# A two-layer encoder trunk on one core: the close of the last tile but one laid over its whole phase, the first norm's parameters expanded two pairs sooner, and the opening norm fed by a broadcast behind x

## The reference, cut to what matters

```
h = layer_norm(x, ln_in_g, ln_in_b)                       # x: 256 tokens x 1024
for i in range(2):
    mix = token_mixers(h, w_in[i], w_out[i], ...)         # differential attention + indexed sparse attention
    h = layer_norm(ALPHA * h + mix, ln1_g[i], ln1_b[i])
    r = ALPHA * h + peer_ffn(h, ...)                      # per token: 8 heads x top 16 of 16384 experts
    gate = sigmoid(r @ ple_wg[i] + ple_bg[i])
    r = r + gate * (p[i] @ ple_wp[i])
    h = layer_norm(r, ln2_g[i], ln2_b[i])
# peer_ffn, per token: act = gelu(u_tab[eidx] . x);  out = sum_k g_k * act_k * v_tab[eidx_k]
```

## Time and profile before

| | |
|---|---|
| median of 3 runs | 1705.87 us (1705.35 to 1707.51) |
| the profiled execution: time | 1710.65 us |
| the profiled execution: span of the core | 1708.8 us |
| PE busy | 1273.0 us (74%) |
| DVE busy | 1071.7 us (63%) |
| POOL busy | 578.6 us (34%) |
| ACT busy | 464.4 us (27%) |
| moved by DMA | 670.38 MB, of which the gathers 536.90 MB |
| mean granted clock of PE | 0.87 |

### The profile page before, as it was taken

How to read it: one execution, slowest core, us unless ns; L and a number is a source line. 1 busy time by engine, 2 the same in 40 slices (tenths; PEclk the granted TensorE clock), 3 DMA queues, 4 the chain that set the end, 5 groups by cost and what they waited for, 6 DMA issues and landing times.

```text
span 1708.8 us, 17975 instructions
## 1 busy us (share of the span) xinstructions
PE 1273.0 (74%) x6232; PEld 590.4 (35%) x6232; DVE 1071.7 (63%) x2754; ACT 464.4 (27%) x1270; POOL 578.6 (34%) x516
## 2 busy tenths in 40 slices
PE   8988767786878798685765979678785885555566
PEld 6655533231542274132531337232352221010112
DVE  1458669664768765555858785663676877555553
ACT  1323223352223323422222422242121342111112
POOL 0003233444322432443334332333333435444430
PEclk9999978988898899798998979968796998767879
DMA  7859999999999999999999999998999989999992
GB/s 254 293 211 407 418 416 402 415 421 418 419 417 419 418 415 417 418 417 419 411 417 421 402 410 415 418 394 341 421 418 418 421 328 420 422 421 421 422 421 116
DMA packets 110522, 670.38 MB, mean 392 GB/s; under 512 B 12240, under 2 KB 12880, under 8 KB 44640
## 3 DMA queue, kind: packets, MB, share of 16 engines
q0 software_dynamic: 73728, 536.90, 76.1%
q1 hardware_dynamic: 36528, 132.20, 19.9%
q10 hardware_dynamic: 176, 0.13, 0.0%
HBM read 668.14 MB, written 1.05 MB: 392 GB/s over the span
## 4 chain that ended last, share of the span: by engine, by line
DMA 40%; PE 32%; DVE 11%; issue 10%; POOL 4%; ACT 3%; POOLq 0%; ACTq 0%; DVEq 0%
DMA rows<-uv_dram,rows_of 34%; PE acc L1231 13%; PE bank L1020 7%; PE bank L1034 6%; DMA wring<-wmix_dram 6%; DVE rows L980 6%; POOL rows L472 4%; ACT dg L644 1%; PE bank L1139 1%; PE bank L1208 1%; PE bank L1131 1%; PE bank L1029 1%; ACT gel L640 1%; DVE i L711 0%; DVE i L702 0%
## 5 line engine op out<-in xcount | busy, mean ns | idle before, releaser
L472 POOL DMA_INDIRECT rows<-uv_dram,rows_of x512 | 578.4, 1130 | 1089.2 <-PE acc L1231 866.5
L980 DVE CUSTOM_DVE_ANT_0 rows<-rows,hx 128x1024 f32<-128x1024 f32 x512 | 621.4, 1224 | 484.3 <-DMA rows<-uv_dram,rows_of 474.0
L1231 PE MATMUL acc<-rows,dg 128*32 128x512 f32 x2048 | 611.2, 733 | 364.9 <-ACT dg L644 364.4
L1231 PEld LDWEIGHTS acc<-rows,dg 128*32 128x32 f32 x2048 | 115.0, 123 | 769.1 <-ACT dg L644 524.1
L640 ACT ACTIVATE gel<-dots 128x2 f32<-128x2 f32 x256 | 51.8, 202 | 817.0 <-DVE dots L980 807.1
L1034 PE MATMUL bank<-wring,xT 128*128 128x512 f32 x384 | 175.3, 601 | 14.4 <-DMA wring<-wmix_dram 13.0
L1020 PE MATMUL bank<-xT,wring 128*128 128x128 f32 x1216 | 148.6, 284 | 10.3 <-DMA wring<-wmix_dram 6.9
L1020 PEld LDWEIGHTS bank<-xT,wring 128*128 128x128 f32 x1216 | 143.6, 198 | 22.1 <-issue 8.1
L644 ACT ACTIVATE dg<-idg,gel 128x32 f32<-128x32 f32 x512 | 136.6, 314 | 24.6 <-ACT gel L640 1.1
L1020 PE MATMUL bank<-qT,wring 128*128 128x128 f32 x896 | 119.4, 295 | 17.8 <-DMA wring<-wmix_dram 17.1
L1020 PEld LDWEIGHTS bank<-qT,wring 128*128 128x128 f32 x896 | 113.0, 208 | 39.9 <-issue 20.4
(11 more groups left out here) (159 smaller groups left out, 932.5 us busy)
## 6 DMA issues: line engine op xcount, KB each, us to landing
wring<-wmix_dram SPq DMA_DIRECT2D x204, 512.0 KB
wring<-wclose_dram SPq DMA_DIRECT2D x30, 512.0 KB
rows<-uv_dram,rows_of POOLq DMA_INDIRECT x512
rows<-wmix_dram SPq DMA_DIRECT2D x8, 512.0 KB, 11.0
rows<-prm_dram SPq DMA_DIRECT2D x2, 1024.0 KB, 10.2
fixed<-fixed_dram SPq DMA_DIRECT2D x1, 576.0 KB, 7.9
res<-x_dram SPq DMA_DIRECT2D x1, 512.0 KB, 4.1
hx<-x_dram SPq DMA_DIRECT2D x1, 512.0 KB, 6.2
```

Source lines behind the costliest of these rows:

```text
L472: pool.indirect_dma_start(out=rows[:, slot, :], out_offset=None, in_=uv_d[phase // TILES], in_offset=bass.IndirectOffsetOnAxis(ap=rows_of[ ...
L980: V.tensor_tensor_reduce(out=rows[:, s, 0:D], in0=rows[:, s, 0:D], in1=hx[:, c, :], scale=1.0, scalar=0.0, op0=ALU.mult, op1=ALU.add, accu ...
L1231: ins = MM(acc[BT * c:BT * c + BT, 512 * i:512 * i + 512], dg[:, s, :], rows[:, s, D + 512 * i:D + 512 * i + 512], start=False, stop=False ...
```

## The change

It has three parts.

Opening. `lnin` (four matmuls, three selectors ahead of it) is gone. The broadcast of the opening norm's gain and shift into `rows[:, 0]`, 1 MB, which stood after `dv1`, is now the second DMA of SP, behind x and ahead of all weights; `embed0` reads it. ACT does the square root of `embed0` before the selectors (`rows`), which are now those of `par` and of the first norm. Two parts with no use of their result are new on PE: `wake`, eight 128x128 matmuls as soon as the identity is there, and `fill`, three 128x512 matmuls between `mix1b` and `h1T`.

First norm's parameters. `gb0` and `gb1` of a mixing run stand at pairs 28 and 29 instead of 30 and 31, and their copy goes to `sc` instead of `probsT`. `mix1a` stands one pair later, behind `mT1`.

Close of CLOSE[2]. In phase 4 each of its pair numbers is taken times three (`close_last`). Both closes of layer 1 now copy `ple` from PSUM into `val`; before, CLOSE[2]'s was read from PSUM. CLOSE[3]'s own `ple` stands at pair 4 instead of 1.

```
-    ("mT0", 30, 31, None), ("gb0", 30, 31, None), ("gb1", 31, 32, None), ("mix0a", 32, None, None), ("mix1a", 32, None, None),
-    ("mT1", 33, 34, None), ("mix0b", 34, None, None), ("mix1b", 35, None, None),
+    ("gb0", 28, 29, None), ("gb1", 29, 30, None), ("mT0", 30, 31, None), ("mix0a", 32, None, None),
+    ("mT1", 33, 34, None), ("mix1a", 33, None, None), ("mix0b", 34, None, None), ("mix1b", 35, None, None),
...
-LAST_EARLY = [("ple", 1, 2, None), ...
+LAST_EARLY = [("ple", 4, 5, None), ...
...
+def close_last(p):
+    return 3 * p
...
-            lay(k, CLOSE_PLAN, CLOSE[k - 2])
+            lay(k, CLOSE_PLAN, CLOSE[k - 2], close_last if k == RUNS else int)
...
             sp.dma_start(res[:], x_d[0]).then_inc(x0_landed, 16)
+            sp.dma_start(rows[:, 0, :], prm_d[P_IN:P_IN + 2, :].rearrange("a d -> (a d)")[None, :].broadcast_to([128, 2 * D])
+                         ).then_inc(lnin_landed, 16)
...
+            def gb_half(run, i):
+                return flat(sc, 512 * i, 512 * i + 512) if run.stage == "mix" else quarter(probsT, i)
...
-                    gain = P_LN1 + 2 * run.layer if n else P_IN
-                    chooser(S_G, gain)
-                    chooser(S_B, gain + 1)
-                    chooser(S_PAR, P_PAR + run.layer).then_inc(rows_ready, 1)
+                    chooser(S_PAR, P_PAR + run.layer)
+                    chooser(S_G, P_LN1 + 2 * run.layer)
+                    chooser(S_B, P_LN1 + 2 * run.layer + 1).then_inc(rows_ready, 1)
...
-                        take(run, name, quarter(probsT, int(name[2])))
+                        take(run, name, gb_half(run, int(name[2])))
...
-                if part == "ple" and run is CLOSE[3]:
+                if part == "ple" and run.layer:
                     for i in range(2):
-                        take(run, f"ple{i}", val[:, 0, 512 * i:512 * i + 512])
+                        take(run, f"ple{i}", val[:, run.tile, 512 * i:512 * i + 512])
...
-                    given = [bank_of(run, f"lnin{i}")[0][:] for i in range(4)]
-                    norm_a([half_of(res, 0), half_of(res, 1)], h, given[0:2], [full_at(run, f"lnin{i}") for i in range(2)])
...
+                    norm_a([half_of(res, 0), half_of(res, 1)], h, params(rows[:, 0, :], 0), [(lnin_landed, 16)])
+                    norm_b(h, params(rows[:, 0, :], D), h_ready)
...
+                if part == "wake":
+                    pe.wait_ge(ident_landed, 16)
+                    for i in range(8):
+                        MM(acc[:, 0:128], ident, ident, start=True, stop=True, skip_group_check=True)
+                if part == "fill":
+                    for i in range(3):
+                        MM(acc[:, 0:512], ident, fixed[:, 128:640], start=True, stop=True, skip_group_check=True)
```

More of the change, by code:

```diff
@@ L174 @@
 ]
-LAST_EARLY = [("ple", 1, 2, None), ("bias", 58, None, None), ("warm0", 60, None, None), ("warm1", 61, None, None),
+LAST_EARLY = [("ple", 4, 5, None), ("bias", 58, None, None), ("warm0", 60, None, None), ("warm1", 61, None, None),
               ("warm2", 62, None, None), ("warm3", 63, None, None)]
@@ L181 @@
 ]
-START_PE = ("lnin T par idx dq0 dq1 dk0 dk1 iw ds0 ix sq0 sq1 dv0 dv1 dpt sk0 dpv sk1 ss0 sv0 sv1 mT0 mix0a mix1a spt0 spt1 spv mT1 "
-            "mix0b mix1b h1T pq0a ps0 pq1a init hx0 ps1 hx1 perm0 pq2a hx2 hx3").split()
-START_ACT = ("rows embed0 T par idx dq1 dk1 iw ix exps0 exps1 sq1 dv1 dpt dpv sk1 rms sexp0 sexp1 sv1 mT0 spt0 spt1 mT1 embed1 n1a "
+START_PE = ("wake T par idx dq0 dq1 dk0 dk1 iw ds0 ix sq0 sq1 dv0 dv1 dpt sk0 dpv sk1 ss0 sv0 sv1 mT0 mix0a mix1a spt0 spt1 spv mT1 "
+            "mix0b mix1b fill h1T pq0a ps0 pq1a init hx0 ps1 hx1 perm0 pq2a hx2 hx3").split()
+START_ACT = ("embed0 rows T par idx dq1 dk1 iw ix exps0 exps1 sq1 dv1 dpt dpv sk1 rms sexp0 sexp1 sv1 mT0 spt0 spt1 mT1 embed1 n1a "
              "h1T pq0a ps0 C0a pq1a hx0 ps1 hx1 hx2 hx3").split()
@@ L859, in part_of @@
                 if part in ("n1a", "n1b"):
-                    buf = rows[:, 1, :] if n == 0 else gb
+                    buf = rows[:, 1, :] if n == 0 else flat(sc, 0, 2 * D)
                 if part == "n1a":
@@ L889, in part_of @@
                     bk, taken = bank_of(run, f"ple{i}")
-                    if run is CLOSE[3]:
+                    if run.layer:
                         dve.wait_ge(*taken_at(run, f"ple{i}"))
-                        V.tensor_tensor(half_of(mixed, i), half_of(mixed, i), half_of(val[:, 0, :], i), ALU.mult).then_inc(L.sem, L.one())
+                        V.tensor_tensor(half_of(mixed, i), half_of(mixed, i), half_of(val[:, run.tile, :], i), ALU.mult).then_inc(L.sem, L.one())
                         settle()
@@ L1047, in part_of @@
                     transposes(run, ["hT0", "hT1"], lambda c: src[:, T * c:T * c + T], [(ready, before + 1), (ready, before + 2)])
[L1048 to L1051, removed]
-                        bk, full = bank(run, name)
-                        MM(bk[:], selrow[:, S_G + i // 2, :], prm[:, 512 * (i % 2):512 * (i % 2) + 512], start=True, stop=True
-                           ).then_inc(full, 1)
+                if part == "wake":
[5 more added lines that the diff above has]
+                        MM(acc[:, 0:512], ident, fixed[:, 128:640], start=True, stop=True, skip_group_check=True)
                 if part == "par":
+                    if n == 0:
+                        pe.wait_ge(prm_landed, 16)
                     pe.wait_ge(rows_ready, n + 1 + max(0, n - 1))
```

2 lines of the change are left out of this document (removed), and 2 rows, old and new, of the table per.

## The result

The changed kernel takes 1692.16 us (median of 4 runs, 1690.59 to 1696.3) where the kernel before took 1705.61 (4 runs): ratio 0.992 (95% interval 0.99 to 0.994), 13.45 us less. The forecast was 1688.9, made of 17.0 us. The profiled execution of the changed kernel took 1696.3, the longest of its four; that of before (1710.65) lies above all four timed runs of before, which end at 1707.51.

What follows compares the result with a forecast made beforehand. DMA was taken as the bound, time being bytes over its rate plus its idle time. Savings of 7.5 + 6.5 + 3.0 = 17.0 us from the median of 1705.87 gave 1688.9, range 1677 to 1700.

Steps and rivals of the forecast that it cites:

- Opening, 7.5: Before the first gather: earlier broadcast, `fill` and `wake` together save 7.5 us.
- The broadcast, 4.5: Opening: broadcast behind x lands at about 7.4, transposes start at 9.7 instead of 14.23, 4.5 us earlier.
- `fill` 3.0: Before h1's transposes: matmuls in PE's idle time save 3.0 us on projection and transposes; bounds 0 and 3.0.
- `wake` 0: Start of PE: raising the clock could save up to 3.7 us; taken as 0, since PE idles again before the transposes.
- Parameters, 6.5: Phase 3: moving `gb0`, `gb1` earlier saves 6.5 of 10.9 us idle DMA; 4.9 at half clock, 10.9 at full.
- How it comes about: Phase 3: `spv` at clock 0.50 (7.09 us), then `gb0`, delay pair 30, and the DMA runs dry.
- Close, 3.0: Head of phase 4: spreading the close saves 3.0 of 9.6 us idle; two whole blocks leave 5.7 at full clock.
- a pair may come 2.5 us late: Price rule for POOL's gathers: a pair's delay up to 2.5 us costs nothing, each microsecond beyond costs one.
- more than that: Rival: `wake` raises the clock and `spv` runs at full clock, 27 us gained, 1679; chance 0.21.
- Only the opening pays: Rival: phase 3 falls back to 0.50 and phase 4's two whole blocks start cold, 1697; chance 0.16.
- the broadcast is late: Rival: broadcast lands at 11.4, the opening gives 3.5, sum 13, 1693; chance 0.07.
- Slower: Rival: all blocks of the spread close run at half clock, 25.6 us lost in phase 4, 1719; chance 0.04.

Runs made afterwards that it cites:

- open_only: The kernel before with only the opening's part of the change (broadcast behind x, `wake`, `fill`, ACT's order); 1697.26 us, ratio 0.9942.
- no_close: The changed kernel without the spread of the close in phase 4; 1697.16 us, ratio 0.9952.
- before_again: The kernel before, unchanged, profiled once more; 1704.05 us in one run.
- dose12: The changed kernel with 96 unused matmuls added to PE in the quiet part of phase 4, in 12 blocks of 8; 1690.02 us, ratio 0.9907.
- no_wake: The changed kernel without the `wake` matmuls ahead of the first transposes; 1692.09 us, ratio 0.9917.
- close_only: The kernel before with only the spread close of phase 4, the `ple` copy into `val` and CLOSE[3]'s `ple` at pair 4; 1699.48 us, ratio 0.9958.
- gb_late: The changed kernel with the first norm's parameters (`gb0`, `gb1`) back at pairs 30 and 31; 1692.41 us, ratio 0.9922.
- lean: split with the first norm's parameters back at pairs 30 and 31 and without `wake`; 1693.94 us, ratio 0.9931.
- split: The changed kernel with its close laid out so that no two blocks stand together, CLOSE[3]'s `ple` at pair 3; 1690.1 us, ratio 0.9908.
- no_fill: The changed kernel without the `fill` matmuls ahead of h1's transposes; 1693.89 us, ratio 0.9929.
- dose3: The changed kernel with the same 96 unused matmuls added to PE in phase 4, in 3 blocks of 32; 1748.33 us, ratio 1.0243.

## Why the prediction was right, and which terms were not

The medians of three kernels, each with one part more, split the gain: before 1705.61, open_only 1697.26, no_close 1697.16, changed kernel 1692.16. That is 8.35 for the opening, 0.1 for the parameters and 5.0 for the close, together 13.45; the prediction had 7.5, 6.5 and 3.0. (Against before of its own batch no_close gained 8.18, which would make the last two -0.2 and 5.3.) That the sum came so near is in part luck: one term was almost wholly wrong, and the two others made up for 2.9 of its 6.4 us.

**Opening, 7.5: right.** The broadcast, 4.5: measured 4.24 and, against before_again, 4.56 us (transposes at 9.99, 14.23 and 14.55); it landed at 7.77 where 7.4 was taken. `fill` 3.0, measured 2.7 by the first gather, 1.7 by the medians. `wake` 0: the medians agree, the mechanism only half. The transposes took 1.23 instead of 1.94 us in four of the eight profiles with `wake` and in none of the six without. Timeline of PE in dose12:

```profile
5.27 3.60 PE L1057 MATMUL acc<-fixed 128*128 128x128 f32 x16 [5.27 <-DMA fixed<-fixed_dram]
10.22 1.23 PE L1016 MATMUL bank<-fixed,h 128*128 128x128 f32 x8 [1.35 <-DVE h L700]
...
12.41 21.32 PE L1026 MATMUL bank<-xT,wring 128*128 128x128 f32 x176
```

By these durations the clock was up at the transposes (the granted clock tells nothing here: it reads 1.00 over the first 10 us in both kinds, even where the matmuls are slow), and the projections start 1.0 us earlier than at 13.44 and end 1.8 earlier. In the four such profiles they end at 33.6 to 33.7 us, in the six others with the early broadcast at 34.9 to 35.6. So in half of the profiles `wake` was worth 1.2 to 2 us of its upper bound of 3.7. That no_wake's median shows none of it stays unexplained. The Trainium skill ("TensorE: Matmul & The Clock Gate", Part 1) says that sustained activity releases the clock at a point that differs from run to run; these profiles agree with it. First gather, over the seven kernels with the whole opening: 115.33 to 120.45, mean 118.5; over the four without: 126.07 to 127.51, mean 126.7. That is 8.2 us, as the medians have it. The 5.6 between the two first profiles is low because the mixing block at 89 us took 8.83 us in one and 7.13 in the other; of the fourteen profiles only before, before_again and dose12 have 7.13.

**Parameters, 6.5: the failed term.** The step was "How it comes about: `spv` takes 7.09 us at clock 0.50": one execution was read as the kernel. With the parameters at pairs 30 and 31 `spv` took 7.09 us in three of six profiles (before, close_only, open_only; not before_again, gb_late, lean). Phase 3 took 408.3 to 412.6 us in the three and 403.4 to 406.1 in the others, 5.2 between the means. With the parameters earlier it took 7.09 in one of eight, dose12:

```profile
1129.86 7.09 PE L1139 MATMUL bank<-val,probsT 128*128 128x64 f32 x32
```

```profile
1139.00:1144.00 5.00, 5.00 (x18) 1.64 (x15) 2.79 (x6) 0.89 (x4) 1.76 (x2) 0.72 0.40 126
```

This is the case that the prediction worked out, the move made and the clock low: it had POOL's gap at 8.9 us and 3.8 us without DMA, dose12 has 8.38 and, added up over windows of 1 us from 1120 to 1180, 3.6. In before, open_only and close_only the same sum is 9.5, 8.0 and 7.9 us, in the ten profiles with `spv` near full clock 0.4 to 1.4. So the mechanism and its price are borne out at the low clock; what failed is that the kernel is there in some of its executions only. Three comparisons of medians give 0.8, 0.1 and 0.25 us, and the means of the same runs 1.3, -0.7 and 0.0; only lean against split hints at more, 3.8, or 3.3 by the means. Whether the move also keeps the clock up, by filling PE's idle times ahead of `spv` (there the matmuls at 1126.25 and 1130.01 now stand), stays open, and so does why three stalls in six profiles leave no mark in the medians. The warning was in the numbers: the profiled execution lay 4.78 above the median, and I carried that difference over to the forecast unchanged instead of asking what in the trace made it.

**Close, 3.0: too small, 5.0.** The mechanism was right, both gaps came where foreseen (8.75 and 10.00). What was mis-sized is what stays, 5.7 us at full clock for the two double blocks: 3.1 for the first with CLOSE[3]'s `ple`, where gb_late, no_wake and no_fill left 3.0 to 3.4 idle, and 2.6 for the second, where they left 0.1 to 0.7 (the changed kernel's own profile, at the low clock, 5.1 and 2.5). In the ledger the time from phase 4 on is 371.5 to 373.9 us with the old close (five profiles), 364.5 and 366.2 with single blocks (split, lean) and 364.7 to 365.4 with double ones at full clock (four profiles), so at full clock the spread is worth 6 to 9 by the ledger. The step "a pair may come 2.5 us late" fails: dose12 makes a pair late by 7.13 - 3.1 = 4.0 us twelve times for nothing. There is no one free gap. At the first double block POOL's gap is 7.75 us in gb_late and the DMA engines run dry 5.9 us after the last issue ended, at about 1365.5; in dose12 the gap is 7.93 us and they never do:

```profile
1360.39 0.94 POOL L481 DMA_INDIRECT rows<-uv_dram,rows_of  x1 [7.93 <-PE acc L1240]
```

```profile
1358.00:1366.00 8.00, 8.00 (x59) 2.81 (x60) 4.49 (x8) 2.74 (x7) 1.98 (x2) 1.00 0.99 395
```

The pair ahead of the block took 3.43 us in gb_late and 1.92 in dose12. Two profiles do not show that this is the reason: dose3's 5.9 us free came behind a pair of 3.63. Double blocks that start at the low clock do cost: 369.1 (changed kernel) and 368.8 us (close_only) from phase 4 on, about half of the gain. The medians, 5.0 and 6.1, stand between.

**The rivals.** Half of *more than that* came true in the profile (`spv` at full clock), without a gain in the medians, since it ran at full clock in three of six profiles without the move as well. *Only the opening pays* fell with no_close, and *the broadcast is late* with the landing at 7.77 us instead of 11.4. *Slower*, the spread close at the low clock, did not happen: in the changed kernel the single blocks ran at 3.70 us, only the starts of the double ones were slow (4.64 and 8.81), and in dose12 the clock was 1.00 through 86 us of added work in small blocks. The forecast of 1688.9 missed by 3.3 us: 6.4 too much for the parameters, against it 2.0 too little for the close, 0.9 too little for the opening, and 0.3 by which the median of before came out lower (1705.61 instead of 1705.87).

## What to carry to other kernels

Before a stall in one profile is priced, ask whether the profiled execution is slower than the median, and whether a second profile of the same kernel shows the stall; this one was in three profiles of six. Where DMA is the bound and a ring of buffers feeds it, as here, price work on a waiting engine by its longest uninterrupted piece and not by its sum: 86 us in pieces of 7 were free, the same matmuls in pieces of 28 cost 56. How long a piece may be is not one number: the DMA engines ran dry 5.9 us after POOL's last issue ended in gb_late, and not in 7.93 us in dose12.

## What the runs showed that I had not expected

- Work added to PE can be free even when it brings it to 100%: dose12, PE busy 100.00 of 100 us, DMA 421 GB/s, median 1690.02.
- One place of one program ran at 1.00 or 0.50 from execution to execution, after idle times of 1.61 and 1.95 or of 1.53 and 2.74 us; `spv` then takes 3.79 or 7.09. The idle times alone do not decide it: after 1.69 and 2.66 us gb_late ran `spv` in 3.79, and dose12 took 7.09 with 0.64 us idle ahead of the pair before it.
- 3.6 to 3.8 us of matmuls at the start came with faster transposes (1.23 instead of 1.94 us) in four profiles of eight.
- A broadcast of 1 MB right behind x landed 6.6 us after its issue; the median of the two in before, among other loads, is 10.2.
